# A two-block model on one core: dense TensorE passes read their tokens and write their accumulator in another order, and the moving operands get another place modulo 512 bytes

## The reference, cut to what matters

```python
z = rms_norm(x, norm1_g) @ w_in            # 1024 -> 2304 (first block), 5 x more in a layer of the second
x = x + mix @ w_out
hf = rms_norm(x, norm2_g) @ w_up           # 1024 -> 2 x 2816
x = x + (gelu(gt) * val) @ w_down          # 2816 -> 1024
x = x + (p @ w_pe) * sigmoid(rms_norm(x, norm3_g) @ w_pg)
```

## Time and profile before

| what | value |
|---|---|
| median of 3 runs | 2549.18 us (2548.86 to 2550.29) |
| the profiled execution | 2548.05 us |
| its span, first to last instruction | 2546.2 us |
| granted TensorE clock, mean | 0.998 |
| PE, PEld busy | 2511.3 us, 2012.3 us |
| DVE, POOL, ACT busy | 1311.4 us, 1512.5 us, 691.6 us |
| HBM read | 218.37 MB |

### The profile page before, as it was taken

The page is one execution under the profiler, slowest core; times in us unless marked ns, Lnnn a source line. Parts: engine busy times, 40 slices in busy tenths (PEclk is TensorE's granted clock), DMA queues, the critical chain, the costliest instruction groups (busy, mean ns, idle before and its releaser), DMA issues.

```text
span 2546.2 us, 47105 instructions
## 1 busy us (share of the span) xinstructions
PE 2511.3 (99%) x16344; PEld 2012.3 (79%) x16344; DVE 1311.4 (52%) x1979; ACT 691.6 (27%) x1290; POOL 1512.5 (59%) x963
## 2 busy tenths in 40 slices
PE   8989999999999999999999999999999999999999
PEld 6868888887877778888888888867678888888887
DVE  7867555465566657663322224566647663322224
ACT  4452000024135446521100002134446531100002
POOL 5666666656646455556666666645454556666665
PEclk9999999999999999999999999999999999999999
DMA  4213222223211122223222223211122223222223
GB/s 167 71 43 119 91 99 99 91 86 117 92 51 52 44 97 69 72 87 103 93 97 99 96 93 122 91 47 50 51 97 67 75 87 103 91 99 95 95 99 99
DMA packets 72442, 222.55 MB, mean 87 GB/s; under 512 B 9312, under 2 KB 12256, under 8 KB 72288
## 3 DMA queue, kind: packets, MB, share of 16 engines
q1 hardware_dynamic: 71856, 220.36, 26.3%
q10 hardware_dynamic: 432, 0.14, 0.0%
HBM read 218.37 MB, written 2.10 MB: 87 GB/s over the span
## 4 chain that ended last, share of the span: by engine, by line
PE 92%; DVE 4%; DVEq 1%; issue 1%; DMA 1%; POOL 1%; ACT 0%; ACTq 0%; POOLq 0%; SPq 0%
PE acc L550 80%; PE bank L550 10%; DMA raw<-in_w_pg 1%; PE bank L1214 0%; POOL w_lo L376 0%; DVE sumsq L1252 0%; DVE y_lo L1252 0%; DVE bank L1252 0%; DVE xg_lo L1345 0%; POOL w_hi L369 0%; DVE bank L1611 0%; DMA vec<-in_vec 0%; DVE att L1464 0%; DVEq L1412 0%; DVEq L1709 0%
## 5 line engine op out<-in xcount | busy, mean ns | idle before, releaser
L376 POOL TENSOR_TENSOR w_lo<-raw,w_hi 128x1024 fp32r<-128x1024 f32 (+3 forms) x438 | 961.8, 2196 | 301.3 <-PE acc L550 242.1
L369 POOL TENSOR_SCALAR w_hi<-raw 128x1024 fp32r<-128x1024 f32 (+3 forms) x438 | 438.2, 1000 | 584.1 <-PE acc L550 503.1
L550 PE MATMUL acc<-xg_hi,w_hi 128*128 128x512 f32 x2208 | 581.8, 397 | 6.7 <-DVE xg_lo L1345 2.9
L550 PE MATMUL acc<-xg_lo,w_hi 128*128 128x512 f32 x2208 | 568.8, 393 | 0.0
L550 PE MATMUL acc<-xg_hi,w_lo 128*128 128x512 f32 x2208 | 562.7, 393 | 0.2 <-POOL w_lo L376 0.2
L550 PEld LDWEIGHTS acc<-xg_hi,w_hi 128*128 128x128 f32 x2208 | 408.6, 188 | 107.1 <-issue 20.9
L550 PEld LDWEIGHTS acc<-xg_hi,w_lo 128*128 128x128 f32 x2208 | 411.3, 188 | 88.4 <-issue 1.5
L550 PEld LDWEIGHTS acc<-xg_lo,w_hi 128*128 128x128 f32 x2208 | 411.2, 188 | 87.4 <-issue 1.5
L2131 ACT ACTIVATE ffn_act<-ffn_t 128x512 f32<-128x512 f32 x100 | 63.2, 632 | 742.6 <-DVEq L1312 600.7
L1252 DVE TENSOR_TENSOR x<-x,acc 128x512 f32<-128x512 f32 x104 | 71.3, 686 | 311.1 <-PE acc L550 310.6
L1252 DVE TENSOR_TENSOR bank<-acc,rstd 128x512 f32<-128x512 f32 x72 | 50.3, 699 | 263.4 <-PE acc L550 263.3
(11 more groups left out here) (351 smaller groups left out, 2708.4 us busy)
## 6 DMA issues: line engine op xcount, KB each, us to landing
raw<-in_w_up SPq DMA_DIRECT2D x132, 512.0 KB, 3.2
raw<-in_w_down SPq DMA_DIRECT2D x48, 512.0 KB, 3.2
raw<-in_w_gate SPq DMA_DIRECT2D x48, 512.0 KB, 3.2
raw<-in_w_ret SPq DMA_DIRECT2D x32, 512.0 KB, 3.3
raw<-in_w_rw SPq DMA_DIRECT2D x28, 512.0 KB, 3.2
raw<-in_w_o SPq DMA_DIRECT2D x48, 256.0 KB, 2.7
raw<-in_w_in SPq DMA_DIRECT2D x18, 512.0 KB, 3.2
raw<-in_w_down SPq DMA_DIRECT2D x24, 384.0 KB, 3.0
```

Source lines behind the costliest of these rows:

```text
L369: nc.gpsimd.tensor_scalar(w_hi[:, s, 0:n], raw[:, s, 0:n], 1.0, 0.0, ALU.mult, ALU.add).then_inc(w_half[s], 1)
L376: nc.gpsimd.tensor_tensor(w_lo[:, s, 0:n], raw[:, s, 0:n], bits(w_hi[:, s, 0:n]), ALU.subtract).then_inc(w_split[s], 1)
L550: return nc.tensor.matmul(o, a, b, start=first, stop=last, skip_group_check=shared)
```

## The change: the order of the columns and the place of the operands

Dense passes go through a new function `dense`, which lays the same map on the moving operand and on the accumulator: the 512 tokens are seen as two halves (h) of 16 runs (r) of 16 tokens (c), and are walked with r from 15 down to 0, under it h from 0 to 1, under it the 16 tokens. The dense moving operands go from 128 to 320 modulo 512 bytes; `raw`, `w_hi` and `w_lo` stay at 128. `z_rt`, `y1`, `y2` and `hid` move with `z_rw`, and so do the tiles of the RWKV mixer, of retention and of attention that are placed behind it. No instruction, DMA or wait is added or taken away.

```diff
-LINE, START = 512, 128
+LINE = 512
+RUN = 16
...
-        xg_hi, _ = place("xg_hi", (DC, T), F32R, line=START)
-        xg_lo, _ = place("xg_lo", (DC, T), F32R, line=START)
+        xg_hi, _ = place("xg_hi", (DC, T), F32R, line=320)
+        xg_lo, _ = place("xg_lo", (DC, T), F32R, line=320)
...
-        raw, _ = place("raw", (2, DC * P), line=START)
+        raw, _ = place("raw", (2, DC * P), line=128)
...
-        y_hi, _ = place("y_hi", (DC, T), F32R, line=START)
-        y_lo, _ = place("y_lo", (DC, T), F32R, line=START)
+        y_hi, _ = place("y_hi", (DC, T), F32R, line=320)
+        y_lo, _ = place("y_lo", (DC, T), F32R, line=320)
...
-        z_rw, rw_at = place("z_rw", (14, T), line=START)
+        z_rw, rw_at = place("z_rw", (14, T), line=320)
...
-        emb_at = base + 24 * 1024 + (START - base) % LINE
+        emb_at = base + 24 * 1024 + (320 - base) % LINE
...
+            def blocks_down(ap):
+
+                return ap.rearrange("p (h r c) -> p r h c", h=2, c=RUN)[:, ::-1]
+
+            def dense(o, a, b, first, last, shared=False):
+
+                return mm(blocks_down(o), a, blocks_down(b), first, last, shared)
...
-                        last = mm(o[:], columns_of(w, s, k), v[:, c, :], v is hi and m == 0 and k == 0, m == 1 and k == n - 1)
+                        last = dense(o[:], columns_of(w, s, k), v[:, c, :], v is hi and m == 0 and k == 0, m == 1 and k == n - 1)
```

More of the change, by code:

```diff
@@ L180, in build @@
         emb, _ = place("emb", (2, T), F32, offset=emb_at + C4)
-        assert {a % LINE for a in (rw_at, rt_at, emb_at)} == {START} and emb_at + 3 * C4 // 2 <= rt_at and base + 4 * sum(int(np.prod(shape)) for _, shape in FIRST) <= emb_at
+        assert emb_at + 3 * C4 // 2 <= rt_at and base + 4 * sum(int(np.prod(shape)) for _, shape in FIRST) <= emb_at
         rw = {}
@@ L587, in late @@
                         pe.sem_inc(pe_turn, 1)
-                        mm(acc[s][:], columns_of(w_hi, s, k), a[0][:, c, :], k == 0, False)
-                        mm(acc[s][:], columns_of(w_hi, s, k), a[1][:, c, :], False, False)
+                        dense(acc[s][:], columns_of(w_hi, s, k), a[0][:, c, :], k == 0, False)
+                        dense(acc[s][:], columns_of(w_hi, s, k), a[1][:, c, :], False, False)
                     pe.wait_ge(w_split[s], I + 2)
@@ L592, in late @@
                     for k, c in enumerate(chunks[:-1]):
-                        mm(acc[s][:], columns_of(w_lo, s, k), a[0][:, c, :], False, False)
+                        dense(acc[s][:], columns_of(w_lo, s, k), a[0][:, c, :], False, False)
                     if stat is not None:
@@ L598, in late @@
                     k, c = n - 1, chunks[-1]
-                    mm(acc[s][:], columns_of(w_hi, s, k), a[0][:, c, :], False, False)
-                    mm(acc[s][:], columns_of(w_hi, s, k), a[1][:, c, :], False, False).then_inc(hi_done[s], 1)
-                    mm(acc[s][:], columns_of(w_lo, s, k), a[0][:, c, :], False, True).then_inc(slot_done[s], 1)
+                    dense(acc[s][:], columns_of(w_hi, s, k), a[0][:, c, :], False, False)
+                    dense(acc[s][:], columns_of(w_hi, s, k), a[1][:, c, :], False, False).then_inc(hi_done[s], 1)
+                    dense(acc[s][:], columns_of(w_lo, s, k), a[0][:, c, :], False, True).then_inc(slot_done[s], 1)
                     return
@@ L606, in late @@
                     pe.sem_inc(pe_turn, 1)
-                    mm(acc[s][:], columns_of(w_hi, s, k), a[0][:, c, :], i == 0, False)
-                    last_hi = mm(acc[s][:], columns_of(w_hi, s, k), a[1][:, c, :], False, False)
-                    last = mm(acc[s][:], columns_of(w_lo, s, k), a[0][:, c, :], False, i == n - 1)
+                    dense(acc[s][:], columns_of(w_hi, s, k), a[0][:, c, :], i == 0, False)
+                    last_hi = dense(acc[s][:], columns_of(w_hi, s, k), a[1][:, c, :], False, False)
+                    last = dense(acc[s][:], columns_of(w_lo, s, k), a[0][:, c, :], False, i == n - 1)
                 last_hi.then_inc(hi_done[s], 1)
@@ L620, in three @@
             def three(s, a, k, first, last):
-                mm(acc[s][:], columns_of(w_hi, s, k), a[0][:, k, :], first, False)
-                hi_pass = mm(acc[s][:], columns_of(w_hi, s, k), a[1][:, k, :], False, False)
-                return hi_pass, mm(acc[s][:], columns_of(w_lo, s, k), a[0][:, k, :], False, last)
+                dense(acc[s][:], columns_of(w_hi, s, k), a[0][:, k, :], first, False)
+                hi_pass = dense(acc[s][:], columns_of(w_hi, s, k), a[1][:, k, :], False, False)
+                return hi_pass, dense(acc[s][:], columns_of(w_lo, s, k), a[0][:, k, :], False, last)
             def hid_slots(I, n, count, ahead=0):
@@ L817, in _ @@
                 w = columns_of(w_hi, 0, c)
-                mm(acc[0][:], w, xg_hi[:, c, :], c == 0, False)
-                last = mm(acc[0][:], w, xg_lo[:, c, :], False, False)
+                dense(acc[0][:], w, xg_hi[:, c, :], c == 0, False)
+                last = dense(acc[0][:], w, xg_lo[:, c, :], False, False)
             last.then_inc(hi_done[0], 1)
@@ L822, in _ @@
             for c in full:
-                last = mm(acc[0][:], columns_of(w_lo, 0, c), xg_hi[:, c, :], False, c == DC - 1)
+                last = dense(acc[0][:], columns_of(w_lo, 0, c), xg_hi[:, c, :], False, c == DC - 1)
                 if c < DC - 1:
@@ L833, in one @@
                 def one(s, w, v, c, first=False, last=False):
-                    return mm(acc[s][:], columns_of(w, s, c), v[:, c, :], first, last, True)
+                    return dense(acc[s][:], columns_of(w, s, c), v[:, c, :], first, last, True)
                 def started(s):
@@ L888, in part @@
                         w, v, c = (w_hi, w_hi, w_lo)[k // DC], (xg_hi, xg_lo, xg_hi)[k // DC], k % DC
-                        last = mm(acc[s][:], columns_of(w, s, c), v[:, c, :], k == 0, k == 3 * DC - 1, True)
+                        last = dense(acc[s][:], columns_of(w, s, c), v[:, c, :], k == 0, k == 3 * DC - 1, True)
                         if k == 2 * DC - 1:
```

## The result

The changed kernel takes **2560.52 us** (median of 5 runs, 2556.78 to 2563.97) against 2549.18 (5 runs, 2548.25 to 2552.15): a ratio of 1.0044, 95% interval 1.0033 to 1.0055. It is slower by 11 us where 95 us less were forecast, and the time lies above the range.

The account below looks back on a forecast made before the run. The pitch of 9456 dense passes, 226.7 ns each, was taken to bound the kernel. Saving 103.1 us less 2.6, 1.6 and 4.2 gave 94.7 us: 2453.4 for the profiled execution, 2454.5 for the median; range 2430 to 2552.

Parts of the forecast that it names:

- What bounds the kernel: Dense passes: 9456 at a pitch of 226.7 ns, of which 13.4 ns is no column.
- The residue: Dense passes: 2.5 ns of loss per pass left after the change, as in fp32 transposes; pitch 215.8, 10.9 ns saved.
- The step that failed: Order of moving columns: twos of runs move 64 bytes down per 13.3 ns, a load passes 64 bytes in 13.4 ns.
- The term of 103 us: All dense passes: 9456 x 10.9 ns = 103.1 us saved.
- the three deductions from it: Savings not reached: gate/embedding pairs 2.6 us, first 210 us 1.6 us, RWKV pairs 4.2 us.
- The bounds of that term: Loss left per dense pass: from 0 (the half-clock passes) to 13.4 ns (nothing gained).
- Modulo 512: Operand places: both runs of a two lie at the same 64 bytes modulo 512; dense operands and weights started at 128.
- Rival 1: Dense passes: the loss is the load's own, a fixed hand-over of 13.4 ns whatever the places; 2549 us, chance 0.14.
- Rival 2: Dense passes: jumps cost more than the streams give back; 2568 us, at the upper bound 2680; chance 0.14.
- Rival 3: Dense passes: the streams still meet and half of the loss stays; 47 us saved, 2502 us; chance 0.10.
- What was costed at nothing: POOL's splits still fit, w_pg pairs stay 7.4 us, DVE frees accumulators in time, other edits cost nothing findable.

## Why the prediction was wrong, step by step

- **What bounds the kernel** held. The pitch is 213.3 + 13.4, and the parts of the 13.4 can now be told apart: 215.8 - 213.3 = 2.5 ns remain beside a load at half the pace, 10.8 come with the full pace. That these 10.8 need the load is not shown: every pass of every run has a load beside it.
- **The residue** was even the right number. Streams at half the full pace do lose 2.5 ns, as the fp32 transposes do. That those went at *the load's* pace was misread: the 0.84 ns of a weight column come from fp32r loads of 188 ns at the full clock. At the half clock (0.50 in the earlier trace rows) the loads take 0.33 us, and those of the transposes 140 ns, so neither shows a load at 0.84 ns a column (the kernel before, a timeline row of PEld, then the group):

```profile
13.18 0.33 PEld L550 LDWEIGHTS acc<-xg_hi,w_lo 128*128 128x128 f32 x1
...
L1214 PEld LDWEIGHTS bank<-ident,an_s 128*128 128x128 f32 x112 | 12.7, 140 | 1.1
```

- **The step that failed** is the one before it: "So the change gives a full-rate pass the load's pace modulo 512." Twos of runs visit places modulo 512 at half speed, but they still read a new column every 0.417 ns, and with that no order went below 226.7 ns, where each column read twice took 215.8. The fp32 and half-clock passes, from which the prediction took 0 to 2.5 ns, read at half the rate in truth. The same rows carried both readings, rate and place, and I took the one that the change could alter. The term of 103 us measured 0 (324.38 us for the 1431 passes, 324.41 before), and the three deductions from it, 8.4 us in all, fell with it.
- **The bounds of that term** failed too. "Nothing gained" was set as the far end, though the earlier trace rows showed 230 ns after a change of order, a sign that other phases cost more. The orders and places measured here lie between 226.7 and 252. This, not the jumps, is the slower side: some 1240 passes at 10 ns more.
- **Modulo 512** was assumed from the code; it is 256.
- **Rival 1** had its sign, "the same 226.7", in 57 of 65 stretches, and its 2549 lies 11.5 us off, but its cause is wrong: with the same load a pass takes 215.8 or 226.7 to 252 ns by what the moving stream reads and where. The rule on ports from the Trainium skill, SBUF — State Buffer, "Who interferes with whom", isn't borne out here: the weights' place alone moves a pass from 226.7 to 233.3 ns.
- **Rival 2** came nearest in time, 2568 against 2560.5, and that is luck: the accumulator's 31 jumps cost nothing (9.68 and 9.90 us with and without), and the operand's jumps cost nothing at its best place. The statement of the Trainium skill, PSUM — Partial Sum Buffer, "Specifications (TRN2)", that any non-contiguous pattern slows matmuls significantly, isn't seen with runs of 16 columns. Its sign, "over 227, in steady stretches, with loads unchanged", did come, from another cause; a sign that two mechanisms share decides nothing.
- **Rival 3**: no stretch settles at 220 to 222. Its other sign, "a pitch that varies", did come, but upward, from 226.7 to 236.7, where half of the loss was to go.
- What was costed at nothing stayed near nothing: POOL, the w_pg pairs, DVE and the small products share the 0.5 us that the account leaves.

What stays open: whether the 10.8 ns need a load, why the loss takes the sizes it takes, and why the change's order has a second beat that the natural order, at its place, never showed in 32 series or in two whole kernels. Also not told apart is whether a start of 340 to 342 ns causes the slow beat or is its first pass.

## What to carry to other kernels

When two streams disturb each other, write down for each how many reads per ns it makes and separately which places it visits; a layout changes only the second, and here only the first went below 226.7 ns. A pitch that depends on a phase should be read stretch by stretch, not as a mean: one number can hide two steady beats, and an edit that leaves the good one alone can add a bad one. A kernel of bare passes tried 76 pairs of order and place in one execution, and would have shown the floor before the change was built.

## What the runs showed that I had not expected

- Whole stretches of identical passes hold one of two beats, 226.7 or 236.7 ns, for hundreds of passes; the two differ by a few ns at their start.
- Across all orders and places many settled beats are one of 226.7, 230.0, 233.3, 236.7 and 240.0, steps of 3.3 ns; 228.3, 229 and 232 occur too.
- Natural reading has a best place of its own, the weights' place modulo 256; 192 bytes off it costs 6.7 ns a pass (2599 us).
- The matched half-rate read reaches 215.8 ns. The Trainium skill, TensorE: Matmul & The Clock Gate, "Back-to-back issue gap", gives N / 2.4 + 2.5 for what it calls the isolated gap, by an estimate from it 215.8 for 512 columns. The trace agrees for that read and for a single column, and not for any other full-rate read of 512 columns in this study, 226.7 at best.
